# Regrouping how the first layer's shift and scale reach its activations, and joining two narrow products

## The chip, the cores and the metric

The kernel runs on one core of one Trainium2 chip. The metric is the device time of one launch in microseconds, the median over runs. Engines are called TensorE (PE in the profile), VectorE (DVE), ScalarE (ACT), GpSimd (POOL) and SyncE (SP). PEld is TensorE's load of stationary operands.

## The reference

The input `x` has 256 tokens of 1024 features, all float32. Two layers of one block come first, then a second block with attention, a recurrent group and a feed-forward part. Only the start of the first block matters here:

```
c_act = silu(c)
shift, scale, gate = split(c_act @ mod_w[i] + mod_b[i], 3)
h = rms_norm(x, norm_g[i]) * (1 + scale) + shift
y = retention(h, ...)            # layer 0: q, k, v, g = split(h @ ret_w_in)
y = forgetting_attention(h, ...) # layer 1: q, k, v, g, f = split(h @ fox_w_in), f is 16 wide
x = x + gate * y
```

`mod_w` is 1024 by 3072 for each layer, so shift and scale of layer 0 alone read 8 MB; the first four column ranges of `ret_w_in` that are used with them read 6 MB.

## The kernel before, in words

**Precision.** Every large product is made in three matmuls: each operand is split into a high part (rounded to the type fp32r) and a low part (the rest). For weights ScalarE writes the high part (`whi`, line 1932 by way of `ring_to`, line 1941) and VectorE the low part (`wlo`, line 1119 by way of `item`, line 1137). Activations stand in `ahi` and `alo`, one column tile `k` (128 features, 256 tokens) after another.

**Items.** `weight_stream` lists everything that SyncE loads in one order, as items of 512 KB in eight buffers `raw`. An item is a weight unit ("u12" is the unit with number 12) or, with the mark "mod", a tile of `mod_w` that VectorE multiplies by `c_act` and adds to `acc` (line 1128). Items 0 to 11 are the units 0 to 11. Item 12 is a mod item, item 13 is unit 12, item 14 a mod item, item 15 unit 13, and so on. VectorE takes them strictly in this order. Its first mod item waits for `acc_in`: two rows of `mod_b` that GpSimd loads into `acc` (lines 2496, 2497).

**The first stage.** For each column tile `k` of layer 0, SyncE loads shift and scale tiles of `mod_w` into the arena (`load_mod`, line 2533). VectorE sums a part of the eight row blocks (`mod_sums`), TensorE adds the others and sums over partitions (`own_rows`, `other_rows`, lines 478 and 484), and VectorE adds the bias (`modulated`). Meanwhile ScalarE has normalised `x` (`normal`), and TensorE turns it (`turn_x0`, line 433). ScalarE then makes `x * scale + shift` (`x0_high`, line 1934) and its high part, and VectorE the low part (`x0_low`). TensorE can then use tile `k`: units 0, 1, 3, 4, 6, 7, 9, 10 (`rows_unit`, lines 529 to 531, 12 matmuls each for one `k`) and units 2, 5, 8, 11 (`products`, lines 392 to 394, 12 matmuls for two `k`). From unit 12 on the products are turned (lines 412 to 414, 24 matmuls of 256 columns for a unit). `SUMMED` says which column tiles have their shift and scale made together: (0), (1), (2, 3), (4, 5), (6, 7).

**GpSimd's queue.** After small loads it waits until the shift and scale of six column tiles stand (`mod0` at 12), and then issues in this order: `positions` into `posi`, `fox_b_f`, a cast, a part of the constants, and the two rows of `mod_b`.

Of the kernel before, what the change touches and what calls it, by code (L numbers as in the profile page):

```python
# [165 lines left out]
SUMMED = [(0,), (1,), (2, 3), (4, 5), (6, 7)]  # L166


VECTOR_ROWS = [4, 4, 6, 6, 6]


def program(nc, x_in, c_in, pos_in, mod_w, mod_b, norm_g, ret_w_in, ret_w_out, fox_w_in, fox_b_f,
            fox_q_gain, fox_k_gain, fox_w_out, final_g, norm1_w, w_in2, lb_logits, hgrn_nw, w_out2,
            norm2_w, w_gate_up, w_down, final_nw, consts, out):
    with ExitStack() as ctx:
# [65 lines left out]
        mod_in = [[(0, 32)], [(1, 32)], [(2, 32), (3, 32)], [(0, 64), (1, 64)], [(2, 64), (3, 64)]]  # L241

        def mod_tile(g):

            n = P * len(SUMMED[g])
            return region((3584, 5632, 7680, 3584, 7680)[g], 16 * n).rearrange("p (a r n) -> p a r n", a=2, r=8)

        def sums_at(k, a):

            return (G[a] if k == 0 else T[a] if k == 1 else T[2 + k % 2])[:, 256 + 32 * a:256 + 32 * a + 32]  # L250
# [26 lines left out]
        zT = PTf[0:16, 0, 0:S]  # L277
# [84 lines left out]
        def _(e):  # L362
# [73 lines left out]
            def keep_warm(n):  # L436

                on_.wait_ge(sig["ones"], 1)
                for _ in range(n):
                    e.matmul(G[2][:, :], warm[:, 0:P], warm, start=True, stop=True)  # L440
# [25 lines left out]
            def turn_x0(k):  # L466

                on_.wait_ge(sig["xn"], 2 if k < 4 else 4)
                on_.wait_ge(sig["h_in"], k - 1)
                transposes(T[2 + k % 2], [xn0[:, m, k * P:(k + 1) * P] for m in range(2)], "x0_turned")  # L470

            def own_rows(g, i, a):

                r0 = VECTOR_ROWS[g]
                o = sums_at(SUMMED[g][i], a)
                for r in range(r0, 8):
                    for c in range(0, P, 32):
                        e.matmul(o[c:c + 32, :], mod_tile(g)[:, a, r, i * P + c:i * P + c + 32], cact[:, r:r + 1].to_broadcast([P, 32]), start=r == r0, stop=False)

            def other_rows(g, i, a):  # L480

                on_.wait_ge(sig["macc"], g + 1)
                for c in range(0, P, 32):
                    d = e.matmul(sums_at(SUMMED[g][i], a)[c:c + 32, :], macc[:, g % 2, a, i * P + c:i * P + c + 32], ones[:, 0:32], start=False, stop=True)
                return d

            def mod_landed(g):
# [5 lines left out]
            def summed(k):  # L493
                for m in range(2):
                    ready[k, m] = (sig["x0"], k + 1)

            def first_sums(g, between=None):

                mod_landed(g)
                for a in range(2):  # L500
                    own_rows(g, 0, a)
                if between is not None:
                    between()
                for a in range(2):
                    d = other_rows(g, 0, a)
                d.then_inc(sig["sums"], 1)
                summed(g)

            def shift_scale(g):

                mod_landed(g)
                for i, k in enumerate(SUMMED[g]):
                    for a in range(2):
                        own_rows(g, i, a)
                        d = other_rows(g, i, a)
                    d.then_inc(sig["sums"], 1)
                    summed(k)
# [18 lines left out]
            def turn_rows():  # L536
                on_.wait_ge(sig["filled"], 1)
                on_.wait_ge(sig["rows_in"], 16 * 9)
                t = bank("rows", sig["rows_read"], 3)
                e.transpose(t[:, 0:P], rows[:, :], idf).then_inc(sig["rows_turned"], 1)  # L540
                turn_x0(0)
                turn_x0(1)
# [7 lines left out]
            for k in range(0, 8, 2):  # L550
                u = 3 * (k // 2)
                if k:
                    rows_unit(u, k)
                rows_unit(u + 1, k + 1)
                if k < 6:
                    turn_x0(k + 2)
                    turn_x0(k + 3)
                products(u + 2, 0, (4, 5, None), k, k == 0, k == 6)
                if k < 6:
                    shift_scale(2 + k // 2)  # L560
                products(u + 2, 1, (4, 5, None), k, k == 0, k == 6)
            for n in range(4):
                g_free[n] = (sig["vh"], n + 1)
            ring[:] = [(sig["sg"], 1), (sig["sg"], 2), (sig["h_in"], 7), (sig["h_in"], 8)]
# [135 lines left out]
            def turn_forget():  # L700
                on_.wait_ge(sig["forget"], 1)
                t = bank("forget_t", sig["forget"], 2)
                for m in range(2):
                    d = e.transpose(t[:, 16 * m:16 * m + 16], zT[:, m * P:(m + 1) * P], idf[0:16, 0:16])
# [21 lines left out]
            nhi, nlo = ahi[:, 29, 0:P], ahi[:, 29, P:2 * P]  # L726
            for k in range(8):
                on_.wait_ge(*ready[k, 0])
                on_.wait_ge(*ready[k, 1])
                wh, wl = nhi[:, k * 16:(k + 1) * 16], nlo[:, k * 16:(k + 1) * 16]  # L730
# [381 lines left out]
        def _(e):  # L1112
# [24 lines left out]
            def item():  # L1137
# [4 lines left out]
                if it[0] == "f":  # L1142
                    on_.wait_ge(sig["narrow_hi"], 1)
                    tt(ahi[:, 29, P:2 * P], raw_tile(n), ahi[:, 29, 0:P].bitcast(F32), ALU.subtract, "used")
# [32 lines left out]
            def mod_sums(g, r0, r1):  # L1177
# [3 lines left out]
                on_.wait_ge(sig["sums"], (0, 0, 1, 2, 4)[g])  # L1181
# [12 lines left out]
            def modulated(k):  # L1194

                on_.wait_ge(sig["sums"], k + 1)
                on_.wait_ge(sig["columns"], 3)
                tt(AB[:, 0, 8 + k:9 + k], sums_of(k, 0), mbc[:, k:k + 1], ALU.add, "mod0")
                ts(AB[:, 0, k:k + 1], sums_of(k, 1), mb1[:, k:k + 1], g_col[:, 0, k:k + 1], ALU.add, ALU.mult, "mod0")

            def x0_low(k):
                on_.wait_ge(sig["h_hi"], k + 1)
                tt(alo[:, k, :], stage0[:, k % 4, :], ahi[:, k, :].bitcast(F32), ALU.subtract, "x0")
# [11 lines left out]
            modulated(0)  # L1215
            ring_to(0)
            x0_low(0)
            copy(gains[:, 1:2], t[:, 53:54], "rows_read")
            ts(gains[:, 0:1], t[:, 52:53], 0.125, None, ALU.mult, None, "rows_read")
            tt(n1f[:, :], t[:, 70:78], n1_col, ALU.mult, "rows_read")  # L1220
            mod_sums(1, 0, 4)
            modulated(1)
            ring_to(1)
            x0_low(1)
            for g in (2, 3, 4):
                k, u = 2 * g - 2, 3 * g - 3
                ring_to(u - 1)
                mod_sums(g, 0, 4)
                mod_sums(g, 4, VECTOR_ROWS[g])
                if g == 2:  # L1230
                    modulated(k)
                ring_to(u)
                if g > 2:
                    modulated(k)
                    modulated(k + 1)
                x0_low(k)
                if g == 2:
                    modulated(k + 1)
                x0_low(k + 1)
                ring_to(u + 1)  # L1240
# [242 lines left out]
            for c in range(4):  # L1483
# [8 lines left out]
                if c == 0:  # L1492
                    on_.wait_ge(sig["forget_pe"], 1)
                    copy(zT, T[bank_of["forget"]][0:16, 0:S], "forget")
# [430 lines left out]
        def _(e):  # L1925
# [15 lines left out]
            def ring_to(u):  # L1941

                while done[0] <= item_of[u]:
# [5 lines left out]
                    if items[n][0] == "f":  # L1949
                        act(ahi[:, 29, 0:P], raw_tile(n), ACT.Copy, "narrow_hi")  # L1950
# [56 lines left out]

            def x0_high(k):

                on_.wait_ge(sig["x0_turned"], k + 1)  # L2010
                on_.wait_ge(sig["mod0"], 2 * k + 2)
                on_.wait_ge(sig["x0"], k - 3)
                act(stage0[:, k % 4, :], T[2 + k % 2][:, 0:256], ACT.Identity, "h_in", scale=col(AB[:, 0, :], k), bias=col(AB[:, 0, :], 8 + k))
                on_.wait_ge(sig["h_in"], k + 1)
                act(ahi[:, k, :], stage0[:, k % 4, :], ACT.Copy, "h_hi")

            normal(0)
            ring_to(0)
            x0_high(0)
            normal(4)  # L2020
            ring_to(1)
            x0_high(1)
            ring_to(2)
            for k in (2, 4, 6):
                ring_to(3 * k // 2)
                x0_high(k)
                x0_high(k + 1)
                ring_to(3 * k // 2 + 2)
# [27 lines left out]
            ring_to(14)  # L2056
            e.dma_start(dec, consts[:, C_DEC:C_DEC + 1536].rearrange("p (h n) -> p h n", h=4)).then_inc(sig["dec_in"], 16)
# [410 lines left out]
        def _(e):  # L2468
# [20 lines left out]
            on_.wait_ge(sig["mod0"], 12)  # L2489
# [40 lines left out]
        def _(e):  # L2530
            on_ = Once(e)

            def load_mod(g):

                n, o = P * len(SUMMED[g]), mod_tile(g)
                on_.wait_ge(sig["mod0"], (0, 0, 0, 4, 8)[g])
# [5 lines left out]
            before = {0: 0, 1: 1, 3: 2, 6: 3, 9: 4}  # L2542
# [40 lines left out]
```

## Time and profile before

| | |
|---|---|
| median of 3 runs | 696.29 us (696.11 to 696.35) |
| profiled execution | 696.31 us |
| its span | 694.5 us |
| TensorE busy | 679.4 us, 98% |
| VectorE busy | 499.8 us, 72% |
| ScalarE busy | 381.3 us, 55% |
| GpSimd busy | 17.3 us, 2% |

Times in the trace count from the start of the span. A matmul's duration contains its run through the array, so that consecutive ones overlap: the step from one start to the next is what each costs in a stream.

### The profile page before, as it was taken

The numbers are of one execution on the slowest core, as the hardware profiler recorded it, in microseconds if no ns is written. First come the engines' busy times: TensorE is split into PE (matmuls) and PEld (weight loads), VectorE is DVE, ScalarE is ACT, GpSimd is POOL, SyncE is SP. The second block draws the span as 40 slices with busy tenths as digits, with TensorE's granted clock in tenths as the row PEclk, the third lists the DMA queues.
The fourth block names the chain that finished last, engine by engine and source line by source line (L and its number), as shares of the span: only waits on it lengthen the run. The fifth ranks groups of instructions, "written<-read, shape, count | busy, mean of one in ns | idle before, by whom it ended". The sixth has DMA issues, their size and how long they took to land.

```text
span 694.5 us, 11561 instructions
## 1 busy us (share of the span) xinstructions
PE 679.4 (98%) x4591; PEld 553.8 (80%) x4591; DVE 499.8 (72%) x803; ACT 381.3 (55%) x561; POOL 17.3 (2%) x35
## 2 busy tenths in 40 slices
PE   7889999999999999999999999999999999999996
PEld 4669997777878888888788877778878888888885
DVE  4788998787986779766768889777665555565445
ACT  5447434565655666554665765845574444444444
POOL 4011000000000000000000000000000000000000
PEclk9999999999999999999999999999999999999999
DMA  9999875667897176833455654433756666655511
GB/s 298 369 377 341 313 247 175 199 225 246 284 350 219 38 243 234 272 124 101 148 153 155 190 171 129 147 122 117 210 160 212 181 188 180 197 185 189 185 60 60
DMA packets 74405, 138.81 MB, mean 200 GB/s; under 512 B 5732, under 2 KB 18400, under 8 KB 74352
## 3 DMA queue, kind: packets, MB, share of 16 engines
q1 hardware_dynamic: 72816, 134.92, 60.4%
q10 hardware_dynamic: 736, 1.81, 0.7%
q0 software_dynamic: 800, 1.35, 0.6%
q8 instruction: 36, 0.59, 0.3%
q14 instruction: 17, 0.14, 0.1%
HBM read 137.01 MB, written 1.05 MB: 199 GB/s over the span
## 4 chain that ended last, share of the span: by engine, by line
PE 88%; DVE 5%; ACT 2%; SPq 2%; DMA 1%; issue 1%; DVEq 0%; ACTq 0%
PE G L392 23%; PE G L394 22%; PE G L393 22%; PE T L433 4%; PE G L412 2%; PE G L413 2%; PE G L414 2%; DVE wlo L1119 2%; PE T L791 2%; DMA arena<-in_mod_w_dram 1%; PE T L779 1%; DVE arena L1128 1%; SPq L2552 1%; SPq L2540 1%; ACT whi L1932 1%
## 5 line engine op out<-in xcount | busy, mean ns | idle before, releaser
L1119 DVE TENSOR_TENSOR wlo<-raw,whi 128x1024 fp32r<-128x1024 f32 x202 | 245.6, 1222 | 111.1 <-ACT whi L1932 110.6
L1932 ACT ACTIVATE whi<-raw 128x1024 fp32r<-128x1024 f32 x202 | 212.2, 1061 | 130.7 <-PE G L394 89.2
L392 PE MATMUL G<-whi,ahi 128*128 128x512 f32 x694 | 280.4, 404 | 0.2 <-DVE wlo L1119 0.2
L394 PE MATMUL G<-whi,alo 128*128 128x512 f32 x694 | 271.0, 391 | 0.0
L393 PE MATMUL G<-wlo,ahi 128*128 128x512 f32 x694 | 270.4, 390 | 0.0
L392 PEld LDWEIGHTS G<-whi,ahi 128*128 128x128 f32 x694 | 130.3, 188 | 29.4 <-issue 1.8
L394 PEld LDWEIGHTS G<-whi,alo 128*128 128x128 f32 x694 | 130.2, 188 | 28.3
L393 PEld LDWEIGHTS G<-wlo,ahi 128*128 128x128 f32 x694 | 130.6, 188 | 25.4 <-issue 1.0
L1934 ACT ACTIVATE arena<-T,st 128x128 f32<-128x128 f32 (+2 forms) x56 | 21.9, 478 | 30.0 <-DVE st L1525 30.0
L1932 ACT ACTIVATE ahi<-T 128x512 fp32r<-128x512 f32 x25 | 15.0, 600 | 39.5 <-PE T L433 39.5
L1934 ACT ACT_TABLE_LOAD x27 | 34.6, 1283 | 3.3 <-issue 1.8
L412 PE MATMUL G<-ahi,whi 128*128 128x256 f32 x128 | 36.4, 284 | 0.0
L413 PE MATMUL G<-alo,whi 128*128 128x256 f32 x128 | 36.2, 283 | 0.0
L414 PE MATMUL G<-ahi,wlo 128*128 128x256 f32 x128 | 36.2, 283 | 0.0
L433 PE MATMUL T<-head,arena 128*128 128x128 f32 x212 | 31.5, 273 | 0.2 <-DVE gate L1119 0.2
L433 PEld LDWEIGHTS T<-head,arena 128*128 128x128 f32 x212 | 25.9, 139 | 7.2 <-issue 0.6
L1128 DVE SCALAR_TENSOR_TENSOR acc<-raw,cact,acc 128x1024 f32<-128x1024 f32 x24 | 30.8, 1282 | 1.0
L1119 DVE TENSOR_TENSOR alo<-T,ahi 128x512 fp32r<-128x512 f32 x25 | 17.3, 691 | 18.0 <-ACT ahi L1932 17.9
L413 PEld LDWEIGHTS G<-alo,whi 128*128 128x128 f32 x128 | 24.6, 192 | 0.0
L412 PEld LDWEIGHTS G<-ahi,whi 128*128 128x128 f32 x128 | 24.5, 192 | 0.0
L414 PEld LDWEIGHTS G<-ahi,wlo 128*128 128x128 f32 x128 | 24.5, 192 | 0.0
L1119 DVE TENSOR_TENSOR arena<-arena 128x512 f32<-128x512 f32 (+7 forms) x46 | 23.0, 546 | 0.8 <-ACT arena L1934 0.5
(254 smaller groups left out, 626.5 us busy)
## 6 DMA issues: line engine op xcount, KB each, us to landing
raw<-in_ret_w_in_dram SPq DMA_DIRECT2D x48, 512.0 KB, 6.4
raw<-in_w_gate_up_dram SPq DMA_DIRECT2D x40, 512.0 KB, 3.8
raw<-in_mod_w_dram SPq DMA_DIRECT2D x32, 512.0 KB, 4.7
raw<-in_fox_w_in_dram SPq DMA_DIRECT2D x32, 512.0 KB, 4.7
raw<-in_w_in_dram SPq DMA_DIRECT2D x28, 512.0 KB, 3.8
raw<-in_w_down_dram SPq DMA_DIRECT2D x22, 512.0 KB, 3.5
arena<-in_mod_w_dram SPq DMA_DIRECT2D x16, 512.0 KB, 9.3
raw<-in_ret_w_out_dram SPq DMA_DIRECT2D x16, 512.0 KB, 5.6
```

The costliest lines, as they stand in the source:

```text
L392: e.matmul(o, ah, wh, start=first and k == 0, stop=False)
L393: e.matmul(o, ah, wl, start=False, stop=False)
L394: done = e.matmul(o, al, wh, start=False, stop=last and k == 1)
L412: e.matmul(o, wh, ahi[:, kt, :], start=first and i == 0 and k == 0, stop=False)
L413: e.matmul(o, wh, alo[:, kt, :], start=False, stop=False)
L414: done = e.matmul(o, wl, ahi[:, kt, :], start=False, stop=last and i == 1 and k == 1)
L433: d = e.transpose(t[:, n * P:(n + 1) * P], s, idf)
L791: d = e.matmul(t[c:c + 64, 65 * a:65 * a + 65], PT[:, g % 2, c0 + c:c0 + c + 64], v[:, j, h, :], start=j == 0, stop=j == m)
L1119: e.tensor_tensor(o, a, b, op).then_inc(sig[name], 1)
L1128: e.scalar_tensor_tensor(out=o, in0=a, scalar=s, in1=b, op0=op0, op1=op1).then_inc(sig[name], 1)
L1932: d = e.activation(o, a, f, scale=scale)
L1934: d = e.activation(o, a, f, scale=scale, bias=bias)
```

## The change

- Shift and scale are made for the column tiles (0, 1), (2, 3), (4, 5), (6), (7). VectorE sums five of eight row blocks in every group, where it was four or six; TensorE does three.
- `x` is turned ahead: four groups of four transposes into the banks G0 to G3 before any shift and scale, and ScalarE copies them into a new SBUF tile `xT`. It lies at 11776 to 13824 of the arena, over `dec` and `posi`.
- `x * scale + shift` is made twice from `xT`: in full by VectorE (`x0_full`), and rounded by ScalarE (`x0_high`), which no longer reads the full tile.
- Since `posi` lies under `xT`, GpSimd's wait ahead of its loads becomes: the low parts of all eight column tiles stand (`x0` at 8).
- In layer 1 the high and low weights of the 16-wide part stand beside each other, so that one matmul with 32 columns replaces two with 16.

```diff
-SUMMED = [(0,), (1,), (2, 3), (4, 5), (6, 7)]
-VECTOR_ROWS = [4, 4, 6, 6, 6]
+SUMMED = [(0, 1), (2, 3), (4, 5), (6,), (7,)]
+VECTOR_ROWS = [5, 5, 5, 5, 5]
@@ tensor
-            first_sums(0, turn_rows)
-            keep_warm(6)
-            rows_unit(0, 0, (0,))
-            on_.wait_ge(sig["rows_read"], 3)
-            first_sums(1)
-            rows_unit(0, 0, (1,))
...
+            turn_x0(0)
+            turn_x0(1)
+            keep_warm(3)
+            turn_x0(2)
+            turn_x0(3)
+            keep_warm(6)
+            shift_scale(0)
+            keep_warm(6)
+            on_.wait_ge(sig["xn"], 8)
+            for k in range(8):
+                u = 3 * (k // 2) + k % 2
+                if k == 7:
+                    rows_unit(u, k)
+                elif k == 6:
+                    rows_unit(u, k, (0,))
+                    shift_scale(4)
+                    rows_unit(u, k, (1,))
+                else:
+                    rows_unit(u, k)
+                if k % 2:
...
+                    products(u + 1, 0, (4, 5, None), k - 1, k == 1, k == 7)
+                    if k < 7:
+                        shift_scale(k // 2 + 1)
+                    products(u + 1, 1, (4, 5, None), k - 1, k == 1, k == 7)
@@ tensor, layer 1
-                e.matmul(t[0:16, 0:S], wh, ahi[:, k, :], start=k == 0, stop=False)
-                e.matmul(t[0:16, 0:S], wl, ahi[:, k, :], start=False, stop=False)
-                d = e.matmul(t[0:16, 0:S], wh, alo[:, k, :], start=False, stop=k == 7)
+                e.matmul(t[0:32, 0:S], ahi[:, 29, 32 * k:32 * k + 32], ahi[:, k, :], start=k == 0, stop=False)
+                d = e.matmul(t[0:16, 0:S], narrow[:, k, 0, :], alo[:, k, :], start=False, stop=k == 7)
@@ vector
+            def x0_full(k):
+                on_.wait_ge(sig["mod0"], columns_made(group_of[k]))
+                on_.wait_ge(sig["xn"], xT_made(k))
+                on_.wait_ge(sig["x0"], k - 3)
+                ts(stage0[:, k % 4, :], xT[:, k, :], col(AB[:, 0, :], k), col(AB[:, 0, :], 8 + k), ALU.mult, ALU.add, "mod0")
...
+            for g, us in enumerate(((0, 1, 2), (3, 4, 5), (6, 7, 8), (9,), (10, 11))):
+                if g:
+                    mod_sums(g, 0, 4)
+                    mod_sums(g, 4, VECTOR_ROWS[g])
+                modulated(g)
+                for k in SUMMED[g]:
+                    x0_full(k)
+                ring_to(us[0])
+                for k in SUMMED[g]:
+                    x0_low(k)
+                for u in us[1:]:
+                    ring_to(u)
@@ scalar
+            def x0_copy(b):
+                on_.wait_ge(sig["x0_turned"], b + 1)
+                act(xT[:, 2 * b:2 * b + 2, :], G[b][:, :].rearrange("p (k n) -> p k n", k=2), ACT.Copy, "xn")
@@ gpsimd
-            on_.wait_ge(sig["mod0"], 12)
+            on_.wait_ge(sig["x0"], 8)
@@ sync
-                on_.wait_ge(sig["mod0"], (0, 0, 0, 4, 8)[g])
+                on_.wait_ge(sig["sums"], (0, 0, 1, 2, 2)[g])
...
-            before = {0: 0, 1: 1, 3: 2, 6: 3, 9: 4}
+            before = {0: 0, 3: 1, 6: 2, 9: 3, 10: 4}
```

## Rows read from the trace of the kernel before

**Rows 1.** What TensorE waited for, whole span (total, times, longest).

```profile
PE G L529 <- DVE alo L1119: 3.2, 4, 1.3
...
PE G L392 <- DVE alo L1119: 0.3, 1, 0.3
```

**Rows 2.** TensorE in order of time (start, duration, instructions, count).

```profile
1.45 3.62 PE L440 MATMUL G<-gate 128*128 128x512 bf16 x9 [1.45 <-DVE gate L1172]
...
10.69 0.30 PE L540 MATMUL T<-head,zmd 128*128 128x128 f32 x1
...
14.24 0.47 PE L529 MATMUL G<-whi,ahi 128*128 128x512 f32 x1 [0.73 <-DVE alo L1119]
...
37.69 0.27 PE L484 MATMUL T<-ones,arena 128*32 128x32 f32 x8 [0.43 <-DVE arena L1128]
...
38.54 0.50 PE L392 MATMUL T<-whi,ahi 128*128 128x512 f32 x1
...
40.83 0.47 PE L529 MATMUL G<-whi,ahi 128*128 128x512 f32 x1 [0.63 <-DVE alo L1119]
...
51.94 0.47 PE L529 MATMUL G<-whi,ahi 128*128 128x512 f32 x1 [0.51 <-DVE alo L1119]
...
60.26 0.28 PE L412 MATMUL G<-ahi,whi 128*128 128x256 f32 x1
...
71.77 0.35 PE L412 MATMUL G<-ahi,whi 128*128 128x256 f32 x1
```

**Rows 3.** VectorE in order of time, the first stage.

```profile
9.80 0.35 DVE L1123 TENSOR_SCALAR arena<-arena,cact 128x256 f32<-128x256 f32 x1 [0.51 <-DMA arena<-in_mod_w_dram]
10.19 1.53 DVE L1128 SCALAR_TENSOR_TENSOR arena<-arena,cact 128x256 f32<-128x256 f32 x3
...
26.60 0.27 DVE L1125 TENSOR_SCALAR AB<-T,mb,cols 128x1 f32<-128x1 f32 x1
26.82 1.23 DVE L1119 TENSOR_TENSOR wlo<-raw,whi 128x1024 fp32r<-128x1024 f32 x1
28.02 0.43 DVE L1119 TENSOR_TENSOR alo<-gate,ahi 128x256 fp32r<-128x256 f32 x1
...
33.66 3.97 DVE L1128 SCALAR_TENSOR_TENSOR arena<-arena,cact 128x512 f32<-128x512 f32 x5
```

**Rows 4.** GpSimd in order of time, around its loads.

```profile
39.57 0.56 POOL L2490 DMA_DIRECT2D arena<-in_positions_dram  x1 [30.82 <-DVE AB L1125]
...
41.94 0.51 POOL L2497 DMA_DIRECT2D acc<-in_mod_b_dram  x1
```

**Rows 5.** DMA issues (queue, count, size, median us to landing), whole span.

```profile
acc<-in_mod_b_dram POOLq DMA_DIRECT2D x1, 4.0 KB, 6.3
gate<-in_mod_b_dram POOLq DMA_DIRECT2D x1, 4.0 KB, 1.9
```

**Rows 6.** VectorE in order of time, from the first mod item to unit 16.

```profile
55.79 1.29 DVE L1128 SCALAR_TENSOR_TENSOR acc<-raw,cact,acc 128x1024 f32<-128x1024 f32 x1
...
57.00 1.22 DVE L1119 TENSOR_TENSOR wlo<-raw,whi 128x1024 fp32r<-128x1024 f32 x1
...
63.28 1.23 DVE L1119 TENSOR_TENSOR wlo<-raw,whi 128x1024 fp32r<-128x1024 f32 x1 [1.15 <-ACT whi L1932]
...
70.45 1.22 DVE L1119 TENSOR_TENSOR wlo<-raw,whi 128x1024 fp32r<-128x1024 f32 x1
```

**Rows 7.** Stretches (us, busy of PE, PEld, DVE, ACT, POOL, granted clock, DMA share, GB/s).

```profile
2.00:6.00 4.00, 4.00 (x14) 1.46 (x13) 0.36 (x1) 1.74 (x3) 4.00 (x9) 1.00 0.93 330
...
40.00:50.00 10.00, 9.08 (x132) 7.22 (x132) 8.62 (x13) 3.96 (x6) 2.45 (x6) 1.00 1.06 381
...
54.00:60.00 6.00, 6.00 (x28) 4.92 (x27) 5.84 (x7) 4.49 (x8) 1.09 (x2) 1.00 0.80 257
...
116.00:117.00 1.00, 1.00 (x6) 0.84 (x5) 0.90 (x5) 0.19 (x2) 0.51 (x1) 1.00 0.00 0
```

**Rows 8.** The narrow products of layer 1 (durations in ns, first and last start).

```profile
L731 PE MATMUL T<-ahi x8: 276/276/281, 242.1 to 244.5; 128*16 128x256 f32 x8
```

More of the change, by code:

```diff
@@ L439, in keep_warm @@
                 for _ in range(n):
-                    e.matmul(G[2][:, :], warm[:, 0:P], warm, start=True, stop=True)
+                    e.matmul(T[3][:, :], warm[:, 0:P], warm, start=True, stop=True)
             keep_warm(9)
@@ L463, in x_ready, with turn_x0 @@
                     ready[slot + k0 + k, m] = (sig["x_split"], 4 * p + (2 + 2 * (k // 2) if n < 4 else 1 + k))
[L466 to L470, printed above, removed]
+            def turn_x0(b):
+                on_.wait_ge(sig["xn"], 2 if b < 2 else 4)
+                transposes(G[b], [xn0[:, m, k * P:(k + 1) * P] for k in (2 * b, 2 * b + 1) for m in range(2)], "x0_turned")
             def own_rows(g, i, a):
@@ L477, in own_rows @@
                     for c in range(0, P, 32):
-                        e.matmul(o[c:c + 32, :], mod_tile(g)[:, a, r, i * P + c:i * P + c + 32], cact[:, r:r + 1].to_broadcast([P, 32]), start=r == r0, stop=False)
+                        e.matmul(o[c:c + 32, :], mod_tile(g)[:, a, r, i * P + c:i * P + c + 32], cact[:, r:r + 1].to_broadcast([P, 32]),
+                                 start=i == 0 and a == 0 and r == r0, stop=False)
             def other_rows(g, i, a):
@@ L491, in mod_landed @@
                     on_.wait_ge(sig[f"mod_in{i}"], n)
[L493 to L512, printed above, removed]
+                for i in range(len(SUMMED[g])):
                     for a in range(2):
                         own_rows(g, i, a)
+                for i in range(len(SUMMED[g])):
+                    for a in range(2):
                         d = other_rows(g, i, a)
-                    d.then_inc(sig["sums"], 1)
-                    summed(k)
+                d.then_inc(sig["sums"], 1)
+                for k in SUMMED[g]:
+                    for m in range(2):
+                        ready[k, m] = (sig["x0"], k + 1)
             def rows_unit(u, k, columns=(0, 1)):
@@ L548, in _ @@
-            first_sums(1)
-            rows_unit(0, 0, (1,))
-            for k in range(0, 8, 2):
-                u = 3 * (k // 2)
-                if k:
-                    rows_unit(u, k)
[L554 to L561, printed above, removed]
+            on_.wait_ge(sig["filled"], 1)
@@ L701, in turn_forget @@
                 on_.wait_ge(sig["forget"], 1)
+                on_.wait_ge(sig["head2_in"], 32)
                 t = bank("forget_t", sig["forget"], 2)
                 for m in range(2):
-                    d = e.transpose(t[:, 16 * m:16 * m + 16], zT[:, m * P:(m + 1) * P], idf[0:16, 0:16])
+                    d = e.matmul(t[:, 16 * m:16 * m + 16], zT[:, m * P:(m + 1) * P], head[0:32, C_SEL:C_SEL + 16], start=True, stop=True)
                 d.then_inc(sig["forget_pe"], 1)
@@ L1180, in mod_sums @@
                 on_.wait_ge(sig["cact"], 1)
-                on_.wait_ge(sig["sums"], (0, 0, 1, 2, 4)[g])
+                on_.wait_ge(sig["sums"], max(g - 1, 0))
                 for r in range(r0, r1):
```

111 lines of the change are left out of this document (49 added, 62 removed).

## The prediction

> **What bounds the kernel now.** I read the list of TensorE's waits first. All but about 1 us of them lie in the first 52 us: the longest total is that of the first-stage products on the low part of an activation, 3.2 us in four waits, and the longest wait of the others is 0.3 us [rows 1]. Then TensorE in order of time: the products of column tile 0 start at 14.24, those of tile 4 at 40.83, those of tile 6 at 51.94, and unit 12 starts at 60.26 [rows 2]. From there TensorE is busy without a hole that matters, up to the end. So there are two questions: when can TensorE start unit 12, and how much work does it have behind that? A third follows from VectorE's order: what stands in front of unit 12 on it [rows 6]?
>
> DMA is not the first limit. From 40 to 50 us it moved 381 GB/s [rows 7]; the seven items of 512 KB for two column tiles (3.67 MB) need 9.6 us of that. A round of two tiles that takes longer than this is set by the engines. The regrouping keeps the bytes; I cost it at nothing there, covered by the difference between 9.6 us and the round worked out below. If that cover were gone, a round could not be shorter than 9.6 us.
>
> **The first products start later.** Prices: an instruction of the shift and scale sums costs 0.021 us on TensorE (40 of them between 37.69 and 38.54 [rows 2]). A 512-column product steps by 0.23 us (36 from 51.94 to 60.26 [rows 2]). On VectorE a summing step costs 0.79 us at 512 elements (3.97 for 5) and 0.51 at 256 (1.53 for 3); a multiplication of 128x256, 0.35; a weight's low part 1.20 from start to next start; an activation's low part 0.43 [rows 3].
>
> The rows transpose stays at 10.69, since it waits for the same nine loads [rows 2]. Behind it now stand 16 transposes of `x` and nine warming matmuls before the first sums. A transpose has no step of its own in these rows; by the narrow product's 0.114 us (2.4 us over 21 steps [rows 8]) it is 1.8 us, and the nine at 0.23 are 2.1 us: 14.6. The first group has 48 + 16 instructions, 1.36 us, and 0.1 us to be seen: 16.05. VectorE's five steps (about 0.5 + 4 x 0.79, from 9.80) and its three copies are over by 14, so they hide.
>
> Then comes a path that I use for every pair: three small operations on the columns 0.5 (26.60 to 26.82 is one step [rows 3]; a third is half of it), two `x0_full` 0.7, one weight's low part 1.20, one activation's low part 0.43, handovers 0.15: **3.0 us**. ScalarE's high parts lie beside it. `x0_full` as such is not in the trace: 0.35 is the 128x256 multiplication with one column; below it is bounded by 0.27 (the same operation form at one element), above by 0.55 if a second column costs as much again as one. This moves a round by 0.4 us at most. So tile 0 starts at **19.05**, 4.8 us later than the 14.24 of before.
>
> **The rounds.** Tiles 0 and 1: TensorE does 30 products (6.9 us), then the next pair's sums (1.36 + 0.1), then waits out the 3.0 us, in which it only has the six products left of the joint unit. That is 11.4 us. Tile 2 starts at 30.4 and tile 4 at 41.8 (before 40.83). VectorE's own work in a round, 3 x 1.20 + 2 x 0.43 + 0.7 + 0.5 + 3.7 = 9.4 us, is less. From tile 4 to 6: 6.9 + a single group's 32 instructions 0.7 + 0.1 + a single path (0.4 + 0.35 + 1.20 + 0.43 + 0.1 = 2.5): **52.0**, level with 51.94.
>
> Here a fifth group costs something that before had no counterpart. VectorE sums tile 7 only after tile 6's low part: 0.35 + 4 x 0.51 = 2.4, to 54.4. TensorE adds 0.3, and another path of 2.5 follows: the low part of tile 7 stands at **57.2**. TensorE's last 24 products of the stage end at 57.2 + 5.5 = 62.7, against 60.26: **+2.4 us**.
>
> **The moved wait.** GpSimd's queue was released at 39.57, and issued its last `mod_b` row 2.37 us later, at 41.94 [rows 4]. Both rows had landed by 48.3 (6.3 us later [rows 5]), long before VectorE's first mod item at 55.79 [rows 6]. Now everything in that queue, five DMAs and a cast, waits for the low part of tile 7: release at 57.2, last row issued at 59.6. VectorE will be at its first mod item at about 58.5 (57.2 + 1.2 for unit 11), and waits there for the row. Queued behind it on VectorE is the low part of unit 12, and TensorE waits for that. ScalarE's high parts and SyncE's raw buffers run full and stop, but they are ahead by then.
>
> The landing time decides. Two rows of this size bound it: 6.3 us in the stretch with a DMA share of 1.06, 1.9 us where the share was 0.00 [rows 5, 7]. In the stretch from 54 to 60 the share was 0.80 [rows 7], and here SyncE issues less, since its buffers wait for VectorE. I take the middle, **4.1 us**: 63.7. A mod item and unit 12 then take 2.43 us (55.79 to 58.22 [rows 6]): unit 12 starts at 66.1, 5.9 us later than 60.26.
>
> VectorE is then level with TensorE instead of 2 us ahead. From the mod item to the end of unit 16's low part it worked 15.88 us with 1.15 us of waiting, so 14.7 us; TensorE needs it 2.43 + 11.51 = 13.9 us after the same mod item [rows 2, 6]. That costs **0.7 us** more. Behind it the units step by 2.88 us (11.51 / 4) and VectorE has 1.2 for a unit plus other work that fitted before.
>
> At this place a rule can be weighed. The trace has 1.9 us for a 4 KB row on idle DMA engines [rows 5]. The Trainium skill, page DMA: Bandwidth & Descriptors, section Anatomy of one DMA, says that a GpSimd transfer has a fixed cost of about 2 us and a part that grows with its bytes. The 1.9 agrees, the 6.3 does not; by the rule alone the row lands at 61.6, and the kernel would take about 699.8 us. This is the third case below.
>
> **The narrow products.** 24 matmuls of 256 columns become 16, in a stretch where TensorE is not waiting. 8 x 0.114 [rows 8] = **-0.9 us**; the 32 rows in place of 16 cost no columns. If VectorE or ScalarE were the limit there, it would be 0; so between 0 and -0.9. The small matmuls that unite the two halves replace two transposes, one for one.
>
> **Sum.** +5.9 + 0.7 - 0.9 = +5.7 us. The profiled execution took 696.31, the median is 696.29: the sum gives 702.0; I say **701.9**. What a measurement of this kernel can tell from no change is about 0.2%, 1.4 us.
>
> **The rivals.**
> 1. *As summed, landing between 3 and 6.3 us*: 700.8 to 704.2. Chance 0.50.
> 2. *The clock falls in the new hole.* TensorE is idle from 62.7 to 66.1. The first nine warming matmuls, after no work, took 0.40 us each (3.62 for 9), against 0.23 later [rows 2]. The granted clock reads 1.00 there, the level of 2.4 GHz [rows 7], yet the pace is nearer to 1.2 GHz. If unit 12 starts like that, nine steps of 0.17 are lost, at most about twice that: +1.5 to 3 us, 703.4 to 705. Against it: holes of up to 1.3 us left the pace alone. Chance 0.12. The Trainium skill, page TensorE: Matmul & The Clock Gate, section What's actually happening, says that the clock halves when the engine has been idle and comes back with work. It would speak for this rival; no row before has a hole of 3 us.
> 3. *A fast landing, near 1.9 us*: -2.2 us, 699.7. It takes DMA engines that are nearly idle at 59.6. Chance 0.17.
> 4. *The row hides, or the front is 2 us shorter than summed*, with a fast landing: what is left is +2.4 - 0.9 or less, 696 to 697.8. Chance 0.14.
> 5. *The other side: TensorE and VectorE don't wait for each other in turn.* If the small groups' columns came back while products still run, a round would be TensorE's own 6.9 + 1.4 + 1.4 = 9.7 us instead of 11.4. Two rounds give 3.4, and the two single paths at the end 2.5 more: tile 7 stands at 51.3, the last row is issued at 53.7 and must land by 57.4, which decides. Unit 12 then starts at 56.8 to 58, with 0.7 and -0.9: 693.5 to 695. For it: holes between the rounds of before were under 1 us each at 40.83 and 51.94 [rows 2]. Against it: the path of 3.0 us is a chain of data, and only 1.4 us of products cover it. Chance 0.07.
>
> **Numbers.** The range takes in rivals 1 and 3 whole, the lower end of 2 and the upper edge of 4: 697.7 to 704.5. Faster by over 0.2% is rival 5 alone, and not all of it: 0.06. Within 0.2% (694.9 to 697.7) is most of rival 4: 0.13. Slower: 0.81.
>
> **What would show it.** Right: first product near 19; `x0` of tile 7 near 57; GpSimd's `positions` load just behind it; a wait of VectorE's first `acc` operation of 3 to 7 us, released by a DMA; a wait of TensorE's first turned product (line 412 of before) of about 3 us; 16 narrow products in 1.8 us. Wrong: if that wait is missing, the landing was shorter or the front earlier; if the rounds are near 10 us, the path of 3.0 us was overlapped; if the first turned products step by more than 0.12 us, the clock fell.

## The result, and the profile after

The changed kernel takes 705.73 us (median of 4 runs, 705.42 to 707.43), the kernel before on the same chip 696.25 us: ratio 1.0141, 95% interval 1.0124 to 1.0159. It is slower by 9.5 us. The prediction said slower, by 5.6 us, and its range ended at 704.5. The profiled execution of after took 705.42 us, its span is 703.5 us, which is 9.0 us more than before.

The list of TensorE's waits, after, whole span (total, times, longest), answers to [rows 1]:

```profile
PE G L532 <- DVE alo L1124: 4.7, 4, 1.6
PE G L429 <- DVE wlo L1124: 4.0, 1, 4.0
PE T L409 <- issue: 1.8, 1, 1.8
```

The first is the wait that was there before, now four times again but for pairs. The second and third are new. The second is the first turned product (line 429; 412 before), held by the low part of unit 12. In the third, TensorE stopped for 1.8 us and the trace shows nothing that it waited for ("issue").

TensorE in order of time, after (start, duration, instructions, count), answers to [rows 2]:

```profile
19.19 0.47 PE L532 MATMUL G<-whi,ahi 128*128 128x512 f32 x1 [1.56 <-DVE alo L1124]
...
27.99 0.40 PE L411 MATMUL T<-whi,alo 128*128 128x512 f32 x1
30.17 0.39 PE L409 MATMUL T<-whi,ahi 128*128 128x512 f32 x1 [1.78 <-issue]
...
30.89 0.63 PE L532 MATMUL G<-whi,ahi 128*128 128x512 f32 x1
31.32 0.63 PE L533 MATMUL G<-wlo,ahi 128*128 128x512 f32 x1
...
43.66 0.47 PE L532 MATMUL G<-whi,ahi 128*128 128x512 f32 x1 [1.38 <-DVE alo L1124]
...
53.89 0.47 PE L532 MATMUL G<-whi,ahi 128*128 128x512 f32 x1 [0.86 <-DVE alo L1124]
...
58.96 0.47 PE L532 MATMUL G<-whi,ahi 128*128 128x512 f32 x1 [0.90 <-DVE alo L1124]
...
64.29 0.39 PE L411 MATMUL T<-whi,alo 128*128 128x512 f32 x1
68.71 0.58 PE L429 MATMUL G<-ahi,whi 128*128 128x256 f32 x1 [4.03 <-DVE wlo L1124]
```

Tile 0 starts at 19.19, where 19.05 was predicted, tile 2 at 30.89 (30.4), tile 4 at 43.66 (41.8), tile 6 at 53.89 (52.0), unit 12 at 68.71 (66.1). The 1.9 us at tile 4 arise in the second round: two consecutive products start 0.43 us apart (30.89 and 31.32), nearly twice the 0.23 that the prediction priced.

What GpSimd and VectorE do in front of unit 12: GpSimd in order of time, which answers to [rows 4], and VectorE, which answers to [rows 6].

```profile
59.11 0.56 POOL L2496 DMA_DIRECT2D arena<-in_positions_dram  x1 [50.36 <-DVE alo L1124]
...
61.48 0.51 POOL L2503 DMA_DIRECT2D acc<-in_mod_b_dram  x1
```

```profile
66.14 1.28 DVE L1133 SCALAR_TENSOR_TENSOR acc<-raw,cact,acc 128x1024 f32<-128x1024 f32 x1 [6.03 <-DMA acc<-in_mod_b_dram]
67.34 1.31 DVE L1124 TENSOR_TENSOR wlo<-raw,whi 128x1024 fp32r<-128x1024 f32 x1
```

The chain that ended last passes through here (start, us, what):

```profile
59.11 0.56 POOL arena L2496
...
61.48 4.58 DMA acc<-in_mod_b_dram
...
67.34 1.32 DVE wlo L1124
...
68.71 0.58 PE G L429
```

So the chain is: low part of tile 7, six instructions of GpSimd (the last one issues the row), one DMA of 4 KB that takes 4.6 us (6.3 before, 1.9 on idle engines [rows 5]), one mod item, one low part, unit 12. VectorE waits 6.03 us for the row. From unit 12 to the end of the span it is 634.79 us (703.5 - 68.71), before 634.24 (694.5 - 60.26).

The granted clock by stretch, after (stretch; busy time of PE, PEld, DVE, ACT, POOL, each with its count; PEclk; DMA share; GB/s), answers to [rows 7]:

```profile
30.17:34.30 4.13, 4.13 (x12) 3.22 (x12) 3.52 (x6) 1.06 (x1) 0.00 (x0) 0.59 1.05 389
68.90:71.80 2.90, 2.90 (x14) 2.90 (x15) 2.80 (x3) 0.00 (x0) 0.00 (x0) 0.51 0.78 278
74.00:78.00 4.00, 4.00 (x36) 4.00 (x35) 3.90 (x7) 2.17 (x3) 0.00 (x0) 1.00 0.97 352
```

Twice TensorE's clock fell from 2.4 GHz (1.00) to 1.2 GHz (near 0.50): behind the stop at 28 to 30, and behind the hole in front of unit 12. From 74 to 78 us it is 1.00.

### The profile page after: what moved, and what is told of

It reads as the page before. It is cut to its first block, busy times and chain, and to the rows that moved or that the text cites. A ratio compares the mean times of both kernels' runs of the same rounds, so it can differ in the third digit from the quotient of the medians.

```text
span 703.5 us, 11703 instructions
## 1 busy us (share of the span) xinstructions
PE 684.2 (97%) x4658; PEld 557.3 (79%) x4658; DVE 499.5 (71%) x807; ACT 379.4 (54%) x557; POOL 17.3 (2%) x35
## 4 chain that ended last, share of the span: by engine, by line
PE 91%; DVE 3%; issue 2%; DMA 1%; POOL 1%; ACT 1%; DVEq 0%; ACTq 0%; POOLq 0%
PE G L409 23%; PE G L411 22%; PE G L410 22%; PE T L450 4%; PE G L429 2%; PE G L430 2%; PE G L431 2%; PE T L796 2%; PE T L784 1%; PE G L532 1%; PE G L533 1%; PE G L534 1%; DMA zmd<-in_fox_k_gain_dram 1%; DVE wlo L1124 1%; DMA acc<-in_mod_b_dram 1%
## 5 line engine op out<-in xcount | busy, mean ns | idle before, releaser
L450 PE MATMUL T<-head,arena 128*128 128x128 f32 x196 | 29.2, 273 | 0.2 <-DVE gate L1124 0.2
L450 PEld LDWEIGHTS T<-head,arena 128*128 128x128 f32 x196 | 23.9, 139 | 6.9 <-issue 0.6
```

Source lines behind the costliest of these rows:

```text
L450: d = e.transpose(t[:, n * P:(n + 1) * P], s, idf)
```

## The experiments

My theory after this result: the moved wait costs most, the later first stage (with its fifth group) some 2 to 3 us, and two falls of the clock the rest. The rivals: the landing would be as late with GpSimd's old wait, since the first stage is busier; and the stop at 28 to 30 belongs to the new tile `xT` or the new order, not to the small matmuls of the shift and scale sums (by the code 64 for a pair: 48 and 16; the profile records each of them twice, and in the fences below `x29` and `x25` count such records). Where a span or a start is given, it comes from that version's profile.

**1. The rows of `mod_b` ahead of the wait.** Only `positions` has to wait for `xT`. So the rows' issue moves in front of GpSimd's wait; the rest of after stays.

```
+            on_.wait_ge(sig["acc_zero"], 1)
+            e.dma_start(acc[0:1, 0:2 * D], mod_b[1:2, 0:2 * D]).then_inc(sig["acc_in"], 16)
+            e.dma_start(acc[0:1, 2 * D:3 * D], mod_b[0:1, 2 * D:3 * D]).then_inc(sig["acc_in"], 16)
             on_.wait_ge(sig["x0"], 8)
...
-            on_.wait_ge(sig["acc_zero"], 1)
-            e.dma_start(acc[0:1, 0:2 * D], mod_b[1:2, 0:2 * D]).then_inc(sig["acc_in"], 16)
-            e.dma_start(acc[0:1, 2 * D:3 * D], mod_b[0:1, 2 * D:3 * D]).then_inc(sig["acc_in"], 16)
```

> The changed kernel with one thing moved: GpSimd issues the two mod_b rows ahead of its wait for the eighth low part, positions and the rest stay behind it. Theory A (the moved wait is most of the loss): VectorE's first acc operation no longer waits 6.0 us for the row; unit 12 starts when TensorE has finished the first stage, near 64.5 instead of 68.7, with no clock drop there, and the kernel takes 705.7 - 4.2 - 1.3 (14 matmuls of unit 12 at half pace, 0.093 us each) = about 700.2 us; positions and the rest land near 65, before VectorE needs them. Theory B (the later front alone is the loss, the wait is hidden): 705.7 as the changed kernel.

Measured: 699.58 us (698.53 to 700.31), ratio 1.0045 (1.0032 to 1.0058), 6.2 us below after. VectorE's wait for the row is gone, and unit 12 starts without a hole:

```profile
64.23 0.28 PE L429 MATMUL G<-ahi,whi 128*128 128x256 f32 x1
64.35 0.28 PE L430 MATMUL G<-alo,whi 128*128 128x256 f32 x1
```

The rows, issued at 9.03 and 9.52, were there long before VectorE wanted them. The first product stood at 20.89 in this profile, 1.7 us later than in after: TensorE had waited 2.17 us for a DMA up to 11.04 (in after 1.15 us), and the granted clock was 0.67 from 12 to 16 us (in after 1.00). The second round lost less, since its stop was 0.79 us and the clock held behind it; unit 12 is 4.5 us earlier all the same. So part of the 6.2 us is the missing fall in the rounds, and not the wait alone.

**2. `xT` elsewhere, so that the old wait is right again.** `xT` over `xn0`, which is read up once turned; ScalarE's copies wait for the transposes that read what they overwrite, and GpSimd waits, as before, for the columns of six tiles.

```
-        xT = region(11776, 2048).rearrange("p (k n) -> p k n", k=8)
+        xT = region(0, 2048).rearrange("p (k n) -> p k n", k=8)
...
-                on_.wait_ge(sig["x0_turned"], b + 1)
+                on_.wait_ge(sig["x0_turned"], 4 if b else 2)
...
-            on_.wait_ge(sig["x0"], 8)
+            on_.wait_ge(sig["mod0"], columns_made(2))
```

> The changed kernel with xT laid over the normalised x, which the transposes have read by then, so that positions no longer lies under it; GpSimd's wait is for the shift and scale of three groups again. ScalarE's first copy waits for two transpose groups, the others for all four, which puts them up to 1 us later. Theory A (the wait is the loss): as with the rows first, 700.2 us, plus 0 to 0.4 for the later copies if they reach the first products. Theory B (the wait is hidden): 705.7. If this one is quicker than the rows-first version, positions and the other loads also held something.

Measured: 698.26 us (697.97 to 699.60), ratio 1.0034 (1.0021 to 1.0046). The products of tiles 0, 4 and 6 and unit 12 start at 19.41, 42.20, 52.41 and 63.03; the stop is there (1.71 us), so it does not come from where `xT` lies, and the clock held behind it. Two rounds take 22.79 us, 11.4 each. From unit 12 to the end it is 633.4 us, 0.87 less than before: that is the narrow products. What is left against before, 2.8 us at unit 12, is the first stage itself. GpSimd issues the last row at 45.79 here, under the old wait; it takes 5.2 us, and VectorE's first mod item at 58.60 does not wait for it: the rival about the landing falls. This run is 1.3 us quicker than run 1, but run 1's late first product covers that, so it doesn't show that `positions` held anything.

**3. Before, with only GpSimd's wait moved.**

```
-            on_.wait_ge(sig["mod0"], 12)
+            on_.wait_ge(sig["x0"], 8)
```

> The kernel before with one line of the change: GpSimd waits for the eighth low part. Theory A: that part stands at 52.7, so the last row is issued at 55.1 and lands after 4.6 us at 59.7; VectorE waits 3.9 us at its first acc operation, unit 12 starts at 62.1 instead of 60.3, and VectorE's lost lead costs up to 0.7 more: 698.2 to 698.9 us, no clock drop since the hole is 2 us. Theory B (the wait is harmful only with the new front): 696.3.

Measured: 699.63 us (698.92 to 700.21), ratio 1.0047 (1.0033 to 1.0061): 3.4 us for one changed line, and 0.7 us above the upper end of what was expected.

```profile
60.63 1.28 DVE L1128 SCALAR_TENSOR_TENSOR acc<-raw,cact,acc 128x1024 f32<-128x1024 f32 x1 [4.64 <-DMA acc<-in_mod_b_dram]
```

```profile
63.10 0.39 PE L412 MATMUL G<-ahi,whi 128*128 128x256 f32 x1 [2.51 <-DVE wlo L1119]
63.32 0.28 PE L413 MATMUL G<-alo,whi 128*128 128x256 f32 x1
63.44 0.29 PE L414 MATMUL G<-ahi,wlo 128*128 128x256 f32 x1
```

The last row was issued at 55.81 and took 4.7 us. Unit 12 is 2.84 us late (63.10 against 60.26), and 0.46 follows behind it, since VectorE is no longer ahead. After a hole of 2.51 us the products step by 0.12: the clock was still 1.00 from 63 to 66. The expectation gave the length of the hole (2 us) as the reason for no fall; no run shows such a limit, and in after a stop of 1.8 us did have a fall behind it.

**4. After, with work in the hole.** In front of unit 12 TensorE waits for a mark that is always set by then, and does 18 warming matmuls into a free bank.

```
+            on_.wait_ge(sig["mod0"], columns_made(1))
+            for _ in range(18):
+                e.matmul(T[2][:, :], warm[:, 0:P], warm, start=True, stop=True)
```

> The changed kernel with 18 matmuls of ones (about 3.9 us) ahead of unit 12, in TensorE's hole from 64.7 to 68.7. Their results are not used. Theory A (the clock drop in the hole costs time of its own): unit 12 still starts at 68.7, but steps by 0.12 us from its first matmul instead of 0.21 for 14 of them; 705.7 - 1.3 = 704.4 us. Theory B (VectorE, which has no lead after its wait, sets the pace of the next units anyway): the start of unit 16 moves by less than 0.5 us and the time stays at 705.2 to 705.7.

Measured: 703.85 us (703.49 to 706.15), ratio 1.0115 (1.0101 to 1.0129). The matmuls filled all but 0.44 us of the hole:

```profile
67.45 0.39 PE L429 MATMUL G<-ahi,whi 128*128 128x256 f32 x1 [0.44 <-DVE wlo L1127]
67.68 0.28 PE L430 MATMUL G<-alo,whi 128*128 128x256 f32 x1
67.80 0.28 PE L431 MATMUL G<-ahi,wlo 128*128 128x256 f32 x1
```

The clock stayed at 1.00, and from unit 12 to the end it is 634.25 us, against 634.79 in after and 635.0 in its repetition (run 8): the fall in the hole costs 0.55 to 0.75 us. The rest above run 2's 633.4, 0.88 us, is put down to VectorE's lost lead (predicted 0.7). The median is 1.9 us below after's and 2.8 below run 8's, much more than that; run 4's profile also has no fall in the rounds, and whether its other executions had fewer of them is not shown.

**5. Four groups.** Run 2 with tiles 6 and 7 made together again.

```
-SUMMED = [(0, 1), (2, 3), (4, 5), (6,), (7,)]
-VECTOR_ROWS = [5, 5, 5, 5, 5]
+SUMMED = [(0, 1), (2, 3), (4, 5), (6, 7)]
+VECTOR_ROWS = [5, 5, 5, 5]
```

> The version with xT over the normalised x (698.3 us, no late row), and column tiles 6 and 7 in one group again, so four groups instead of five. Theory A (the fifth group adds a second path of 2.5 us and 2.4 us of sums at the end): the last pair is a round like the others, tile 6 starts at 42.2 + 11.4 = 53.6 instead of 52.4, but then all 36 products of the stage run through: unit 12 at 53.6 + 8.3 = 61.9 instead of 63.0, 697.2 us. Theory B (the groups' number costs nothing, the late start of the first products is the whole loss of the front): 698.3.

Measured: 698.59 us (697.38 to 698.90), ratio 1.0030 (1.0018 to 1.0041), like run 2. By run 2's rounds unit 12 should have come at 42.2 + 11.4 + 8.3 = 61.9; it came at 63.68. The profile has a longer stop and then the clock at half:

```profile
30.77 0.59 PE L409 MATMUL T<-whi,ahi 128*128 128x512 f32 x1 [2.23 <-issue]
31.16 0.63 PE L410 MATMUL T<-wlo,ahi 128*128 128x512 f32 x1
...
44.16 0.47 PE L532 MATMUL G<-whi,ahi 128*128 128x512 f32 x1 [1.37 <-DVE alo L1120]
```

So this run did not settle what the fifth group costs; it showed that the stop and the fall are not particular to after.

**6. Before, with only the narrow products joined** (the diff's layer 1 part alone, with the small matmuls that unite the two halves).

> The kernel before with the joined narrow products alone. Theory A (TensorE sets the pace there, 8 matmuls of 0.11 us are saved in full): 696.25 - 0.9 = 695.4 us. Theory B (hidden behind VectorE or ScalarE): 696.25.

Measured: 695.97 us in 11 runs (695.57 to 696.35), ratio 0.9994 (0.9985 to 1.0003). The interval contains no change. The profile has 633.5 us from unit 12 to the end, 0.75 less than before, but unit 12 itself stood 0.45 later. The saving behind unit 12 is seen twice (0.87 in run 2); in the time it is at the limit of what can be measured.

**7. Run 5 without the nine warming matmuls ahead of the first sums.**

```
             turn_x0(1)
-            keep_warm(3)
             turn_x0(2)
             turn_x0(3)
-            keep_warm(6)
             shift_scale(0)
```

> The four-group version without the 3 + 6 warming matmuls ahead of the first sums. Theory A (TensorE's own queue ahead of the first sums sets the start of the first products): the sums come 9 x 0.23 = 2.1 us sooner, but not before VectorE's part at 13.4, so about 1.9 us: first products at 17.5, unit 12 at 60.0, 695.3 us. Rival: without them the clock falls at the start and the first products step by 0.43 us for 3 us, which gives back 1 to 1.5 us: 696.5.

Measured: 696.36 us in 12 runs, but from 695.0 to 700.43; ratio 1.0010 (0.9995 to 1.0024). The first product is 1.6 us earlier (17.79). Theory A's time (695.3) came in two of the 12 executions (695.00, 695.27). The profiled execution is the longest of the 12: a stop of 2.55 us inside the third group's sums, and a slow stretch behind it.

```profile
39.97 0.41 PE L501 MATMUL T<-ones,arena 128*32 128x32 f32 x25 [2.55 <-issue]
...
43.36 0.76 PE L532 MATMUL G<-whi,ahi 128*128 128x512 f32 x1 [0.82 <-DVE alo L1118]
```

Its mean granted clock over the span was 0.994; the execution of 695.0 us had 0.999. The stop is a round later than in run 5, with nine matmuls fewer ahead of it.

**8. After once more**, unchanged.

> The changed kernel once more. In its first profile the clock was at its lower level from 30.2 to 34.3 us, behind a hole of 1.8 us; in two versions with the same rounds it was not, and their tile 6 started 1.4 us earlier. Theory A (this fall comes and goes with the run): runs spread by 1.4 us or more, from about 704 to 707.5, and this profile may show the rounds at 11.4 us each. Theory B (it belongs to this kernel): the fall is there again at the same place.

Measured: 706.66 us (703.94 to 707.54), ratio 1.0142 (1.0126 to 1.0157). The profile has the stop (1.71 us) but no fall behind it, so tile 4 starts at 42.05 and tile 6 at 52.24, as predicted (41.8, 52.0), and tile 7's low part ends at 57.17 (57.2). The hole in front of unit 12 is the same, and the clock fell behind it again:

```profile
67.08 0.39 PE L429 MATMUL G<-ahi,whi 128*128 128x256 f32 x1 [4.04 <-DVE wlo L1124]
```

```profile
31.00:34.00 3.00, 3.00 (x15) 2.49 (x14) 2.55 (x4) 1.06 (x1) 0.00 (x0) 1.00 1.05 398
68.00:69.00 1.00, 1.00 (x6) 1.00 (x6) 1.00 (x2) 0.00 (x0) 0.00 (x0) 0.50 0.82 307
```

Unit 12 comes 1.63 us earlier than in after's first profile. The first stage's fall comes and goes from execution to execution. That makes about 1.6 us of the 3.6 by which after's eight executions differ (703.94 to 707.54). Five of them took 705.99 us or more, and none of those has a profile. Their mean granted clocks are 0.991 to 0.995, those of the two profiled executions 0.995, so most had more of the lower clock; where, is not shown.

**9 and 10. The number of small matmuls.** Run 2 with VectorE summing seven of the eight rows in groups 1 to 4, so that TensorE has 32 small matmuls for a pair in place of 64, and with four rows ([5, 4, 4, 4, 4]), which makes it 80.

```
-VECTOR_ROWS = [5, 5, 5, 5, 5]
+VECTOR_ROWS = [5, 7, 7, 7, 7]
```

> The version with xT over the normalised x (five groups, nine warming matmuls), with VectorE summing seven of eight row blocks from the second group on, so that TensorE's burst of small matmuls for a pair falls from 64 to 32 instructions. In the runs so far TensorE stops for 0.8 to 2.6 us with nothing that releases it, right behind or inside such a burst, while the DMA share is above 1; after some of these stops the clock is at its lower level for 4 us. Theory C (the stop comes from the burst: TensorE's instructions are used up faster than they are brought in): the stop is gone or below 0.5 us, the clock stays, rounds are the larger of TensorE's 10.7 and VectorE's 11.0 us, unit 12 starts at 62 to 62.5 instead of 63.0, runs spread by under 1 us, 697.4. Theory D (the stop is tied to the time or to something else): it stays at 1.7 us and the spread of 1.6 us with it, 697.4 to 698.5.

> The other way: VectorE sums four of eight row blocks from the second group on, TensorE's burst for a pair grows to 80 instructions. Theory C: stops grow to 2.5 us or more or come in more groups, the clock falls in most runs; rounds of 11.4 + 0.34 us, and with a fall + 1.4: 699 to 702, against 698.3. Theory D: 698.3 + 3 x 0.34 = 699.3, spread as before.

Run 9: 698.36 us (698.22 to 698.43), ratio 1.0030 (1.0019 to 1.0042); no stop, and a spread of 0.2 us over six runs, where run 2 had 1.6. Theory C's signs came, its time (697.4) did not: VectorE's longer sums now hold tile 7 (TensorE waits 1.43 us for them), and unit 12 starts at 63.05 instead of 62.5 or less. Run 10: 701.86 us (701.62 to 703.48), ratio 1.0085 (1.0072 to 1.0097), with a stop of 1.59 us within the second pair's sums and a round of 13.3 us (20.96 to 34.29). Theory C's time came (699 to 702), its mechanism only in part: the stop did not grow to 2.5 us, and the clock held behind it. And 1.5 us of its time is the first product, which came as late as in run 1 (20.96), with a wait of 2.19 us up to 11.11 ahead of it.

```profile
30.86 0.45 PE L501 MATMUL T<-ones,arena 128*32 128x32 f32 x29 [1.59 <-issue]
```

**11 and 12. Both together.** Run 7 (four groups, no warming ahead of the sums, `xT` over `xn0`) with seven rows ([5, 7, 7, 7]), and with six, which is 48 small matmuls for a pair, as before had.

```
-VECTOR_ROWS = [5, 5, 5, 5]
+VECTOR_ROWS = [5, 6, 6, 6]
```

> The four-group version without warming matmuls ahead of the first sums (696.4 us, runs from 695.0 to 700.4), with VectorE summing seven of eight row blocks from the second group on. Theory C: no stop, no fall, so its runs lie together; first products at 17.8, rounds of 11.0: unit 12 at 17.8 + 33.0 + 8.3 + 0.3 = 59.4, 60.3 - 0.9 before: 694.6 us. Theory D: median 696.4 with the same spread of 5 us.

> As the last one with six of eight row blocks on VectorE, bursts of 48 instructions, as many as in the kernel before. Theory C: stops of under 1 us at most, no fall in most runs, rounds of 11.1 us: 694.9 us, spread under 2 us. Theory D: 696.4 us with a spread of 5 us.

Run 11: 695.85 us (694.89 to 696.25), ratio 0.9991 (0.9982 to 1.0000). Beside run 9, which has the same rows, unit 12 starts 3.36 us earlier (59.69 for 63.05), and 1.33 of that is the earlier first product (17.78 for 19.11): the other 2.03 is what the fifth group costs at seven rows. Run 12: 694.45 us in 11 runs (694.09 to 695.70), ratio 0.9982 (0.9973 to 0.9991): the interval leaves out no change, but 0.18% is less than the 0.2% that the prediction trusted a measurement to tell. Neither profile has a stop. In run 12's the rounds are 11.0 us each and the clock is full:

```profile
17.78 0.47 PE L532 MATMUL G<-whi,ahi 128*128 128x512 f32 x1 [1.73 <-DVE alo L1118]
...
28.75 0.47 PE L532 MATMUL G<-whi,ahi 128*128 128x512 f32 x1 [1.38 <-DVE alo L1118]
...
39.76 0.48 PE L532 MATMUL G<-whi,ahi 128*128 128x512 f32 x1 [1.38 <-DVE alo L1118]
...
50.74 0.47 PE L532 MATMUL G<-whi,ahi 128*128 128x512 f32 x1 [1.38 <-DVE alo L1118]
...
58.99 0.28 PE L429 MATMUL G<-ahi,whi 128*128 128x256 f32 x1
```

```profile
17.78:28.75 10.97, 9.60 (x133) 7.52 (x133) 9.68 (x17) 4.47 (x7) 0.00 (x0) 1.00 1.07 367
28.75:39.76 11.01, 9.63 (x133) 7.52 (x133) 9.50 (x17) 4.05 (x6) 2.09 (x3) 1.00 1.07 367
```

Unit 12 starts 1.27 us earlier than before.

## Why the prediction was wrong on the time and right on the direction

**The account of the 9.0 us**, from the spans and the starts of unit 12. The first stage, with the old wait and the full clock: 2.8 (run 2, 63.03 - 60.26). The moved wait: 4.05 (runs 8 and 2, 67.08 - 63.03). The clock's fall in the first stage: 1.6 (after against run 8). Behind unit 12: -0.87 for the narrow products, +0.88 for VectorE's lost lead, +0.55 for the clock behind the hole. That is 9.0. The prediction had +2.4, +3.4 (66.1 - 62.7), 0, -0.9, +0.7, 0 and thus 5.7 (from rounded terms 5.6).

**What held.** The first product (19.19 for 19.05), and the rounds of 11.4 us on the mean wherever the clock held: two rounds took 22.8 us in run 2. So rival 5 (rounds near 10 us) did not occur, and neither did rivals 3 and 4, a fast landing or a shorter front. The first stage's +2.4 us, put down to the fifth group, measured 2.8, and the group itself 2.0 (runs 9 and 11, at seven rows). The moved wait is the largest cost: run 3 shows it by itself, and runs 1 and 2 take it back. The narrow products gave 0.87 behind unit 12 for 0.9. The lost lead was 0.88 for 0.7. The signs that were named came: `positions` right behind tile 7's low part, an `acc` wait between 3 and 7 us (6.03), a wait of line 412's counterpart, though of 4.0 us instead of 3, and 16 narrow products in 1.7 us.

**The step that failed: "A 512-column product steps by 0.23 us", taken for every product of the rounds.** In after's second round it stepped by 0.43 until 34.3. The prediction counted a clock that stays, because no hole before had taken it away; it did not count the stop of 1.8 us that the larger burst of small matmuls brings, nor the fall behind it. This is 1.6 of the 3.4 us by which the profiled execution exceeded the sum, and with the 0.55 of the second fall it is what took the time out of the range. Such a stop alone costs little (a first round of 11.6 us in run 8, 11.2 in run 7, which had no stop there), because TensorE would have waited for VectorE anyway: tile 4 in runs 2, 4 and 8 is at 42.05 to 42.20 with stops of 1.7 us. A stop inside the sums, where VectorE waits for them, is paid: run 10's round with it took 13.3 us, the next 11.5.

**Rival 2 happened as well as rival 1, not in its place.** The prediction gave the fall behind the new hole a chance of 0.12 and no share in the sum. It fell in both profiles of after. Its size was over-estimated (1.5 to 3 us against the 0.55 to 0.75 that run 4 gives): the units run at half pace for 3 us, but VectorE sets their pace in that stretch too, and TensorE at half pace falls only a little behind it. "Holes of up to 1.3 us left the pace alone" was true, but 2.5 us did too (run 3), 4.0 us did not in either profile, and of four stops of 1.7 to 1.8 us one was followed by a fall (runs 2, 4 and 8 had none), as were those of 2.2 and 2.6 us (runs 5 and 7), while those of 0.8 and 1.6 us were not (runs 1 and 10). The Trainium skill, page TensorE: Matmul & The Clock Gate, section What's actually happening, says that the clock is halved by idleness and given back by work. After's rows agree (0.51 behind the hole, 1.00 from 74 on). The prediction named it and still gave the rows of before more weight, although none of them had such a hole.

**A term that was too small: the landing.** 4.1 us was the middle of 1.9 and 6.3; 4.6 was measured in after and run 8, 4.7 in run 3 and 5.0 in run 4. This is 0.5 of the 3.4. The rest of the 3.4 is the 0.55 of the second fall, 0.4 in the first stage, 0.2 in VectorE's lead, 0.1 more in the moved wait, and roundings. A fixed cost of about 2 us, which the Trainium skill states on the page DMA: Bandwidth & Descriptors, section Anatomy of one DMA, fits only the row on idle engines (1.7 us in after's trace); the 4 KB row in a busy stretch took 4.6 to 6.3 us in the profiles of before, after and the runs, so the measurement decides.

**The range.** Its top, 704.5, was little more than the dearer landing alone (704.2). But a dear landing, a fall behind the hole by the prediction's own lower figure and a fall in the rounds can come together: 704.2 + 1.5 + 1.6 = 707.3, where the 1.6 is known only from the runs. After's executions go up to 707.5, but that they are made up so is not shown.

**Why TensorE stops.** With 64 small matmuls or more for a pair there was a stop of 0.8 to 2.6 us in all eight such profiles; with 48 (before, runs 3, 6 and 12) or 32 (runs 9, 11) there was none. Such a group is 64 matmuls by the code; the profile records 128, each with a weight load, in 1.23 us (26.20 to 27.43 in after). The profile's instruction queue q8 carried 37 packets, 0.61 MB, so 16 KB each, for the 9,316 matmuls and weight loads of TensorE: one packet for some 250.

Two things in the traces tie a packet to the stop. First its place: counting recorded matmuls and weight loads together, the 706th is the one that starts late in seven of the eight profiles, whatever stands there (a product in after, a small matmul in run 10), and in run 7 it is the 962nd, exactly 256 further. Second its time: in all eight, that instruction starts 1.4 to 1.6 us after a q8 packet ends. In after the packet begins at 27.69 and takes 1.09 us (DMA of the stretch 27.6 to 27.8 us: packets, MB, share of 16 engines; a packet's time counts where it begins):

```profile
q8 instruction: 1, 0.02, 34.1%
```

It ends at 28.78, and TensorE goes on at 30.17. In the six profiles without a stop the 706th comes at 32.5 us or later, 2.9 us or more behind the packet near 28 us. So a late block of instructions is the reading that all 14 profiles bear out, and more small matmuls bring TensorE to the block's edge sooner. It fits too that the first pair's sums, as large, brought no stop: the edges before are the 194th, at 15.3 us in after, and the 450th, at 26.2, and the packet between them ended at 20.3, 5.9 us ahead of the second. The Trainium skill, page Runtime: NRT & Kernel Launch, section Instruction fetch mechanics, describes such blocks of 16 KiB with 256 instructions and calls their cost mostly hidden; the 256 agrees with the distance above, the cost here was not hidden. What fell short is proof by experiment: no run shifted the block's edge and nothing else.

**What stays open.** Why a packet begins only near 28 us in every profile, and why the clock falls behind a stop in some executions only. Nor was the fifth group's cost with five rows isolated, since run 5 was disturbed by the fall; the 2.0 is for seven rows.

## What to carry to other kernels

When a buffer's new place makes a wait stricter, cost everything that stands behind that wait in its queue, not only the load that needs it: here two rows of 8 and 4 KB that had no tie to the buffer made up about half of the loss, and moving their issue ahead of the wait gave most of it back. Sum a range's rivals before fixing its top, since a late transfer opens a hole and a hole can take the clock. Where two engines share a sum, the split changes more than its busy time: six rows of eight instead of five cost VectorE 0.8 us for a pair, by the price of a summing step, and was the steadier and faster choice (run 12 against run 7). And count TensorE's instructions as well as its time: by the reading above, a dense group of small ones brought it to instructions that had not arrived.

## What the runs showed of the hardware that was not expected

- TensorE stopped without a releaser for 0.8 to 2.6 us shortly after, or in, the 64 or 80 small matmuls of a later pair, where the DMA share was over 1; with 48 or 32 it did not. It went on at its 706th or 962nd recorded instruction, 1.4 to 1.6 us after a 16 KB packet of its instruction queue had ended.
- The granted clock fell from 2.4 to 1.2 GHz behind both holes of 4.0 us, not behind one of 2.5 us, and behind stops of 1.7 to 2.6 us in some executions only. In runs 1 and 10 it was at 0.67 and 0.68 from 12 to 16 us, behind a wait of 2.2 us up to 11 us (1.0 to 1.9 us in the other versions of after, which had no fall there), and the first product came 1.5 to 1.7 us later. A fall in the rounds cost 1.6 us, one behind the hole 0.55 to 0.75.
- GpSimd's cast of 128x128 to bf16 took 0.30 us in before and after, where VectorE was idle (in before but for the first 0.03 us), and 3.57 us in runs 2 and 12, where it lay beside an unbroken row of VectorE's low parts and ended 0.15 us after them (run 12: 42.37 and 42.22; run 2: 44.80 and 44.65):

```profile
38.80 3.57 POOL L2493 CAST idb<-head 128x128 bf16<-128x128 f32 x1
```
